# Both one-hots of the gate spreading for eight tokens in one operation each, the gates multiplied in by a third, and three tiles of products after the last token

## The reference, cut to what matters

```python
def block(tb):
    q = jnp.einsum('pd,de->pe', tb, wq).reshape(-1, PEER_HEADS, 2, half)
    s = jnp.einsum('phik,hink->phin', q, subkeys).astype(jnp.float32)
    s1, i1 = lax.top_k(s[:, :, 0], PEER_TOPK)
    s2, i2 = lax.top_k(s[:, :, 1], PEER_TOPK)
    cand = (s1[..., :, None] + s2[..., None, :]).reshape(s1.shape[0], PEER_HEADS, -1)
    cidx = (i1[..., :, None] * PEER_NKEYS + i2[..., None, :]).reshape(s1.shape[0], PEER_HEADS, -1)
    top_s, pos = lax.top_k(cand, PEER_TOPK)
    idx = jnp.take_along_axis(cidx, pos, axis=-1)
    gate = jax.nn.softmax(top_s, axis=-1)
    ue = jnp.take(table_u, idx, axis=0)
    ve = jnp.take(table_v, idx, axis=0)
    act = jax.nn.gelu(jnp.einsum('pd,phkd->phk', tb, ue).astype(jnp.float32), approximate=False)
    return jnp.einsum('phk,phkd->pd', (gate * act).astype(tb.dtype), ve)
```

## Time and profile before

| | us |
|---|---|
| median of 3 runs (4368.73 to 4369.26) | 4368.85 |
| the profiled execution | 4368.09 |
| its span | 4366.3 |
| PE busy, whole program | 3848.4 (88%) |
| DVE busy, whole program | 2488.9 (57%) |
| the stage `spread_gates` in the span | 2886.3 to 3157.8 |

### The profile page before, as it was taken

One profiled execution on the slowest core, in us unless ns is written; L12 is line 12 of the kernel. 1 busy time (PEld: TensorE's weight loads), 2 busy tenths in 40 slices (PEclk: granted clock), 3 DMA queues, 4 the chain that ended last, 5 costly groups with the idle time before them and its releaser, 6 DMA issues. The chain is left out here.

```text
span 4366.3 us, 50841 instructions
## 1 busy us (share of the span) xinstructions
PE 3848.4 (88%) x19207; PEld 3090.7 (71%) x19207; DVE 2488.9 (57%) x4067; ACT 1522.4 (35%) x2294; POOL 873.7 (20%) x445
## 2 busy tenths in 40 slices
PE   6989989978999588888889979979799999999995
PEld 3768966448888577776645538867688788888884
DVE  2647860137777377777710038999755454545454
ACT  3424321034555244455510023346522232323231
POOL 0220002003333011111111004422144221212120
PEclk8989999989999789999989989989999999999997
DMA  4111003311110111111032323325655333333331
GB/s 179 42 39 36 24 20 111 133 70 39 49 44 30 41 39 40 45 48 39 25 149 87 125 88 111 116 96 189 211 205 194 132 124 118 125 115 128 112 131 47
DMA packets 135463, 403.35 MB, mean 92 GB/s; under 512 B 16369, under 2 KB 55137, under 8 KB 125665
## 3 DMA queue, kind: packets, MB, share of 16 engines
q1 hardware_dynamic: 135264, 400.68, 26.6%
HBM read 348.18 MB, written 52.45 MB: 92 GB/s over the span
## 5 line engine op out<-in xcount | busy, mean ns | idle before, releaser
L2654 POOL TENSOR_TENSOR ex_vl<-ex_v,ex_vh 128x1024 fp32r<-128x1024 f32 x80 | 191.9, 2399 | 685.7 <-ACT ex_vh L2642 685.7
L2638 ACT ACTIVATE ex_ab<-ps 128x512 f32<-128x512 f32 x80 | 47.8, 598 | 611.3 <-PE ps L346 611.3
L344 PE MATMUL ps<-ex_xh,ex_ul 128*128 128x512 f32 x640 | 250.1, 391 | 9.8 <-DVE ex_ul L2661 9.8
L344 PE MATMUL ps<-hT_high,ma_wl 128*128 128x384 f32 (+1 forms) x576 | 233.7, 406 | 24.9 <-DVE ma_wl L3599 24.9
L2680 DVE TENSOR_TENSOR ex_acc<-ex_acc,ps 128x512 f32<-128x512 f32 x160 | 109.8, 688 | 248.0 <-PE ps L346 248.0
L1822 DVE TENSOR_TENSOR mg_sg<-mg_sg,ps 128x512 f32<-128x512 f32 x32 | 22.0, 688 | 399.8 <-PE ps L1771 365.4
L346 PE MATMUL ps<-ex_xh,ex_uh 128*128 128x512 f32 x640 | 249.7, 390 | 0.0
L345 PE MATMUL ps<-ex_xl,ex_uh 128*128 128x512 f32 x640 | 249.7, 390 | 0.0
L344 PE MATMUL ps<-ex_vh,ex_al 128*128 128x512 f32 x640 | 249.0, 389 | 0.0
L345 PE MATMUL ps<-ex_vl,ex_ah 128*128 128x512 f32 x640 | 249.0, 389 | 0.0
L346 PE MATMUL ps<-ex_vh,ex_ah 128*128 128x512 f32 x640 | 249.0, 389 | 0.0
(11 more groups left out here) (539 smaller groups left out, 10401.1 us busy)
## 6 DMA issues: line engine op xcount, KB each, us to landing
ex_u<-in_peer_u SPq DMA_DIRECT2D x80, 512.0 KB, 4.2
ex_v<-in_peer_v SPq DMA_DIRECT2D x80, 512.0 KB, 4.1
gates_by_expert<-sg_gbuf SPq DMA_DIRECT2D x8, 4096.0 KB, 15.1
ma_w<-in_w_in_ma SPq DMA_DIRECT2D x48, 512.0 KB, 3.6
ev_v<-in_peer_v SPq DMA_DIRECT2D x48, 512.0 KB, 3.5
hg_w<-in_w_in_hg SPq DMA_DIRECT2D x40, 512.0 KB, 3.5
ex_g<-gates_by_expert SPq DMA_DIRECT2D x20, 1024.0 KB, 4.8
mg_wg<-in_w_merge SPq DMA_DIRECT2D x16, 1024.0 KB, 4.9
```

The lines of the kernel that those rows point to most:

```text
L344: pe.matmul(out, a[1], b[0], start=start, stop=False)
L2638: act.activation(ab[:, j % 2, :], ps[:, j % 2, :], ACT.Gelu).then_inc(h_read, 1)
L2654: pool.tensor_tensor(vl[:, j], v[:, j % 2], vh[:, j].bitcast(F32), ALU.subtract).then_inc(vl_ready, 1)
```

## The change

In `spread_gates` DVE now works on eight tokens at a time (64 groups). Three TENSOR_TENSORs of 128x1024 take the place of ten instructions: the comparison for `two`, the comparison for `one`, and the multiplication of `two` by the gates, in place. The third waits on a new semaphore for the first. `hot_ready` counts groups of eight, and PE waits for `n // 2 + 1`; DVE waits until PE is done with the group that used the same buffers, two groups back. `steps_to` spreads 17 tiles (136 steps) over the quads, and PE does the steps of the last three tiles after the last quad. ACT's and SP's lists follow `steps_to` with the same code.

```diff
@@ -2104,6 +2104,7 @@
 EARLY_GROUPS = 12
 ROUTE_TILES = 28
+LAST_TILES = 3
...
-        steps_to = lambda n: KD * count * n // quads
+        steps_to = lambda n: KD * (count - LAST_TILES) * n // quads
...
             @block.vector
             def _(dve):
-                for n in range(quads):
-                    if n >= OH // 4:
-                        dve.wait_ge(g_done, n - OH // 4 + 1)
-                    t0 = 4 * n % OH
-                    dve.tensor_tensor(one[:, t0:t0 + 4, :], iota.unsqueeze(1).to_broadcast([P, 4, P]),
-                                      chosenT[:, 0, 4 * n:4 * n + 4].unsqueeze(2).to_broadcast([P, 4, P]), ALU.is_equal)
-                    for a in range(4):
-                        t = 4 * n + a
-                        ins = dve.tensor_scalar(two[:, t0 + a, :], iota, chosenT[:, 1, t:t + 1], chosenT[:, 2, t:t + 1],
-                                                ALU.is_equal, ALU.mult)
-                    ins.then_inc(hot_ready, 1)
+                for n in range(quads // 2):
+                    if n >= 2:
+                        dve.wait_ge(g_done, 2 * (n - 1))
+                    t0, t = 8 * n % OH, slice(8 * n, 8 * n + 8)
+                    each = lambda a: chosenT[:, a, t].unsqueeze(2).to_broadcast([P, 8, P])
+                    wide = iota.unsqueeze(1).to_broadcast([P, 8, P])
+                    dve.tensor_tensor(two[:, t0:t0 + 8, :], wide, each(1), ALU.is_equal).then_inc(second_ready, 1)
+                    dve.tensor_tensor(one[:, t0:t0 + 8, :], wide, each(0), ALU.is_equal)
+                    dve.wait_ge(second_ready, n + 1)
+                    dve.tensor_tensor(two[:, t0:t0 + 8, :], two[:, t0:t0 + 8, :], each(2), ALU.mult).then_inc(hot_ready, 1)
...
                 for n in range(quads):
-                    pe.wait_ge(hot_ready, n + 1)
+                    pe.wait_ge(hot_ready, n // 2 + 1)
...
                     for _ in range(steps_to(n + 1) - steps_to(n)):
                         next(ahead, None)
+                for _ in ahead:
+                    pass
```

More of the change, by code:

```diff
@@ L2334, in spread_gates @@
         gbuf = sb("sg_gbuf", [P, 2, PEER_KEYS, TG])
-        steps_to = lambda n: KD * count * n // quads
+        steps_to = lambda n: KD * (count - LAST_TILES) * n // quads
         with core.stage(f"w_in*{W}", "high_ready", "low_ready", "tile_done", "tile_read", "h_ready", "h_stored*3",
-                        "hot_ready", "g_done", "g_read", "g_stored*2") as (
+                        "hot_ready", "second_ready", "g_done", "g_read", "g_stored*2") as (
                 block, w_in, high_ready, low_ready, tile_done, tile_read, h_ready, h_stored,
-                hot_ready, g_done, g_read, g_stored):
+                hot_ready, second_ready, g_done, g_read, g_stored):
             @block.sync
```

## The result

| | us, median (lowest to highest, runs) | against before, same chip [95%] |
|---|---|---|
| before | 4369.26 (4368.73 to 4370.84, 5) | 1 |
| after | 4389.97 (4389.33 to 4391.76, 5) | 1.0048 [1.0033, 1.0062] |

What follows compares the result with a forecast made beforehand. DVE was taken to bound the gate-spreading loop, the last gate store its end. DVE +8.1, clock +4 and end +3.0 made 15.1 us on the profiled 4368.09, 4383.2, or 4384.0 as median; range 4368 to 4402.

Steps and rivals of the forecast that it cites:

- DVE's one-hots: Gate-spreading loop: 192 wide operations starting 1.14 us apart take 218.9 us, 10.3 more than the old one-hots without stalls.
- The stalls: DVE's loop: each of 19 POOL subtractions before the last one-hot costs DVE 2.1 us, 39.9 in all.
- The faster rival: DVE's loop: wide operations and POOL's subtraction pass each other, all 42 us of stalls go; -28.8 us, 4340; chance 9%.
- The sum for DVE: DVE's loop: one-hots 218.9 plus stalls 39.9 make 258.8 us against 250.7 before, +8.1.
- The clock, +4 us: PE in the loop: 2.3 us waits fell its clock at five of sixteen places, DVE standing 0.8 us at each.
- The end, +3.0: After the last one-hot: three tiles left on PE outlast the gates' store, next stage after 23.8 us instead of 20.8.
- The change does nothing, because PE is the bound: Rival for the loop: no effect as PE sets the pace; rejected since DVE idles 0.15 us in 250.8; no chance given.
- Pauses and more falls: Rival for the loop: pauses at the third operation's new wait, clock falls at most places; +32 us, 4401; chance 12%.
- pauses at all three operations: Variant of the pauses rival: a pause before each of a group's three operations, 23 us in the loop; 4407.
- The clock holds: Rival for PE in the loop: full clock through the 2.3 us waits; +11.1 us, 4380; chance 16%.
- no measurable change: Rival for DVE's loop: stalls of 1.5 us each and no clock fall; -0.3 us, half-way to it 4374; chance 13%.
- The prediction's bracket: PE's idle waits: one of 1.38 us did not fell the clock, one of 2.42 us elsewhere did.

Runs made afterwards that it cites:

- wide_chained: The changed kernel with a group's first two operations exchanged, so the third waits for the one just before it; 4398.52 us, 1.0068 to before.
- wide_deep: The changed kernel with one-hot buffers for 32 tokens instead of 16, so DVE may run four groups ahead instead of two; 4389.20 us, 1.0046 to before.
- the pair without POOL: The kernel before, and the changed kernel with two tiles last instead of three, each with POOL's subtraction moved to DVE; 4349.75 and 4363.21 us.
- wide_short_sub: The changed kernel with POOL's subtraction cut to 128 of 1024 columns from the fourth tile on; 4353.31 us, 0.9962 to before.
- old_last_tiles: The kernel before with only the three last tiles put after the last token; 4370.17 us, 1.0000 to before.
- old_short_sub: The kernel before with POOL's subtraction cut to 128 of 1024 columns from the fourth tile on; 4349.70 us, 0.9953 to before.
- wide_all_tiles: The changed kernel with all 20 tiles spread over the tokens again (LAST_TILES = 0), the wide one-hots alone; 4384.21 us, 1.0032 to before.

## Why the prediction was right, and where it was off

Slower was right, and 4390.0 lies within 4368 to 4402, 6 us above the 4384.0. The loop took 268.4 us, more than the 259 to 264 given as the sign of the forecast. By its steps:

- **DVE's one-hots, 218.9 us at 1.14 each.** Right: starts are 1.14 apart, the third operation's wait opens no pause (wide_chained shows what one would cost), and the pair without POOL gives 218.1, a cost of 9.4 us for the 10.3 in the sum.
- **The stalls, 19 x 2.1 = 39.9.** Right: 257.6 busy less 218.9 leaves 38.7 (39.5 by the 218.1 above), and the long instructions are all of wide TENSOR_TENSORs, 3.41 us at most. The faster rival, that they pass POOL, is dead. The sum for DVE, 258.8, was off by 1.2.
- **The clock, +4 us.** The mis-sized term. It was built on 16 separate waits of PE of 2.3 us, one per subtraction, five of which fell the clock for 0.8 us of DVE's time each. What ran is 10.6 us of DVE waiting for PE: 2.4 at the start, where the prediction waved its three places away because PE waits for the first tile anyway, and 8.2 in eight waits behind falls of the clock. The number of falls (six) was near the five. But only two were of the kind foreseen, after 2.15 us, and they cost 1.0 and 0.7 us. The other single subtractions left PE standing for 1.45 to 2.16 us, less than the 2.3 foreseen, and left the clock alone. At the four others POOL, kept out until the next tile was ready or nearly so, did two or three behind each other, PE stood 4 to 5 us, the clock was low for up to 6.8 us, and DVE lost up to 1.96 us each, 6.5 in all. That the number of falls came out near the guess is luck: it was a choice between none and sixteen, for waits of another kind. That an unbroken DVE keeps POOL out for 23.8 us was not foreseen: POOL was said to cost 2.1 us, and not asked what it would do itself. wide_deep, where the same thing grows to 35.6 us, and wide_short_sub, where it costs little, show that the place is right, and wide_chained, where DVE waits only behind the stands that fell the clock, that the price is the clock's.
- **The end, +3.0.** It is +4.1. PE's 16.6 us and the eviction came as worked out (20.5 us after the last one-hot, 20.6 predicted), and the gates' store was covered. The last tile's store landed after 2.0 us, sooner than the 2.3 of the earlier trace rows. The mis-sized term is the last one, 0.1 us for the barrier: from the landing to the next stage it is 1.7 us. It was so before too, where the gates were issued at 3142.21 and landed 13.9 us later, and the next stage began at 3157.82; the prediction had this 1.7 within its 15.6 for the gates and left it out for the tiles. old_last_tiles shows the term in another light: in the old kernel the loop is 1.5 us shorter with 17 tiles in it, which nearly pays it back.
- **The rivals.** "The change does nothing, because PE is the bound" is false here; PE sets part of the old kernel's pace only once POOL's part is gone (old_short_sub). "Pauses and more falls" at 4401 had the waits right in kind, not the pauses; the chained kernel built it and gave 4398.5. Its price for pauses at all three operations, 4407, leaves out the 9 us for falls that the 4401 has; with them it would be 4416. "The clock holds" is out by the six falls, "no measurable change" by stalls of 2.0 us each.

What lets POOL in at last is open, but the traces show a regularity. `steps_to` spreads 136 steps over 128 quads, so behind every sixteenth quad PE does two steps instead of one and frees the buffers of the next eight tokens later. The DVE groups that wait for just these are the groups 10, 18, 26 and so on up to 58, counted from 0. In after all five subtractions that stood more than 4 us after the start got in at such a group (10, 26, 34, 50, 58), and in wide_short_sub all seven that stood that long within the loop (10, 18, 26, 34, 42, 50, 58). In wide_all_tiles PE does two steps behind every fourth quad, so every even group is of this kind: all 17 subtractions after the start came in at even groups, and none stood over 6.8 us. If these groups are the openings, LAST_TILES = 3 made them rarer. But it isn't shown that PE's later release is the cause: at groups 50 and 58 it still came 1.7 us before DVE's operation began. In wide_chained, which has a pause in each group, the entries lie at all three operations alike (means 1385, 1423 and 1450 ns).

Why PE's pauses of 1.8 to 2.3 us fell the clock in some cases and not in others is left unexplained.

## What to carry to other kernels

Count what an engine streams before how often it is told to: 448 instructions fewer cost 9.4 us here, because a multiply that rode along in a two-operation instruction became a pass of its own. Where GpSimd shares data work with a DVE that is the bound, price its work by what it takes from DVE (here 2.1 us for 2.4 of its own, against 1.14 when DVE does it itself), and try it on DVE. And a DVE list made smoother, or given deeper buffers, can keep GpSimd out, as it did here: look at the longest of GpSimd's instructions, not at the median.

## What the hardware showed beyond that

- With DVE's two-input instructions 1.14 us apart and nothing between them, GpSimd's 2.4 us subtraction stood up to 23.8 us, and 35.6 in wide_deep; with 64 pauses of 0.12 us, never over 3.4. The Trainium skill, SBUF — State Buffer, section Who interferes with whom, says that such a pair contends for a port and that the order of issue decides who is blocked. That they contend, the trace agrees: 2.1 us for DVE. That GpSimd, once ready, is passed by some eleven later instructions of DVE (2916.3 to 2929.2), the order of issue alone does not say.
- PE's pauses of 1.23 to 1.49 us left the clock at 2.4 GHz in all 18 cases of wide_all_tiles. Those of 1.81 to 2.29 us took it down to 1.2 in nine of 13 cases of wide_chained, those of 1.82 to 1.98 in three of nine of old_last_tiles, and those of 1.93 to 2.16 in two of four of after. The prediction's bracket (1.38 no, 2.42 yes) holds, but within it the length of the pause alone does not decide.
